# A gate table from one 256-column product per token, gate banks taken before the maximum, and 20 early expert pairs in a two-layer encoder kernel

## The chip, the cores and the metric

The kernel runs on one core of a Trainium2 chip. The metric is the device time of one execution in microseconds (us); before the change it is 2279.7 us, the median of three runs (2278.73 to 2285.3). The engines are named as the profile names them: PE is TensorE, PEld its weight loads, DVE VectorE, ACT ScalarE, POOL GpSimd, SP SyncE, which here only starts DMAs.

## The reference

Two layers over 256 tokens of width 1024, in float32. Each layer has three attention mixers whose outputs are gated and added, and then an expert layer (PEER). The change touches the expert layer most:

```python
def peer(xn, wq, subkeys, u, v):
    q = (xt @ wq).reshape(T, PEER_HEADS, 2, PEER_HALF)
    s = jnp.einsum('thpc,phnc->thpn', q, subkeys)
    top_s, top_i = lax.top_k(s, PEER_TOPK)                      # 16 of 128 keys, twice
    cand_s = top_s[:, :, 0, :, None] + top_s[:, :, 1, None, :]
    cand_i = top_i[:, :, 0, :, None] * N_KEYS + top_i[:, :, 1, None, :]
    best_s, best_pos = lax.top_k(cand_s.reshape(T, PEER_HEADS, 256), PEER_TOPK)
    expert = jnp.take_along_axis(cand_i..., best_pos, axis=-1)  # one of 128 x 128
    g = jax.nn.softmax(best_s, axis=-1)
    hid = jax.nn.gelu(jnp.einsum('td,thkd->thk', xb, u[expert]))
    return jnp.einsum('thk,thkd->td', g * hid, v[expert])
```

The first half of a layer is one projection into q, k, v and gate logits, differential attention (A), band attention (B) and stick-breaking attention (C), `sum_i sigmoid(G_i) * (y_i @ P_i)` and an output projection.

## The kernel before, in words

**Experts as a dense table.** The kernel does not gather experts. It computes the hidden value of all 128 x 128 experts for all 256 tokens and multiplies them by a gate table G[first key (partition), second key, token] that holds the softmax weight of a chosen expert and zero elsewhere. Second keys are worked in 64 pairs; the weights of a pair come as four slots of 128x1024 (two from `w_u`, two from `w_v`).

**Products in halves.** Every big product runs on operands split into a rounded high part and the remainder (type fp32r): `product` (L482 to L486) does hi x hi, lo x hi and hi x lo. So each weight slot is loaded by SP into `raw`, rounded by ACT into `w_hi` (L925, L1107) and subtracted by DVE into `w_lo` (L1253, L1637) or by POOL (L463, L469). There are four slots (`SLOTS`); SP loads a slot again when its w_lo is made.

**The stages of a layer**, each on all engines at once with semaphores (`Signal`, with a count per layer) between them: transposes of x and its gain; 36 projection slots with the C mixer's work and head norms fitted in between (three tables named `between`, one each for PE, ACT and DVE, keyed by slot); 24 gate slots in 16 steps of attention work (two and one in turn, `STEP_SLOTS`); up and output projections; query and scores; then the experts.

**The gate stage.** In step i PE does a gate slot, the score of i + 2, the transposes of probabilities i, in even steps a second gate slot, and mix i - 1 (L687 to L697). On DVE a step is `probabilities(i)`, `score_max(i + 2)` and then `after_gates(i - 1)`, which does the splits of the step's slots and `take_gate` (L1402), the product of a gate bank with rstd. The PE's gate slot waits until the bank two gates before has been taken. All of this runs in the order in which it is written.

**The expert stages.** While DVE chooses the top keys (L1553 to L1608), PE does `EARLY` = 18 pairs with `w_u`; their gelu goes straight into G. Then comes the fill stage of `FILL` = 32 pairs, in which PE alternates one slot of a pair (24 products) with one `gate_group` of four tokens (64 groups in all). For a group DVE builds two rows of 128 zeros and ones for each token (`make_hot`, L1643), ACT multiplies one of them by the token's weight (`weigh_hot`, L1172, four instructions), PE multiplies the two (L801, f32, 128x128 for each token), DVE multiplies the columns whose hidden values stand already in G (`keep`, L1652), and ACT copies the rest (`take_group`, L1186). The gelu of the pair follows (L1198, L1200) and `weigh_fill` (L1661). The 14 late pairs do `w_u` and `w_v` in turn, the remaining 50 (`KEPT`) only `w_v`.

**Between the layers** DVE adds the output to x in four tiles (L1736), PE transposes them, DVE applies the gain (L1262), ACT rounds (L935) and DVE subtracts (L1270); the first product of the layer needs that. At the start of the program SP loads x tiles 0 and 1, and ACT, once tile 1 is there, tiles 2 and 3 (L898 to L900).

## Time and profile before

| | before |
|---|---|
| median of three runs | 2279.7 us |
| profiled execution, its own time | 2281.6 us |
| its span, first to last instruction | 2279.9 us |
| PE busy | 2223.6 us (98%) |
| DVE busy | 1557.9 us (68%) |
| ACT busy | 1175.7 us (52%) |
| POOL busy | 252.1 us (11%) |
| mean granted clock of PE | 0.995 |

Busy time is the union of an engine's instructions; on PE it is modelled from starts, so the starts tell more than the durations. The idle time of PE, some 56 us, is put down to the instruction that released it. A granted clock of 1.00 is 2.4 GHz, 0.50 is 1.2 GHz. The timeline gives each instruction's start and duration; "x4" merges neighbours of one kind, and the value in brackets is the engine's idle time before.

### The profile page before, as it was taken

The numbers are of one execution on the slowest core, as the hardware profiler recorded it, in microseconds if no ns is written. First come the engines' busy times: TensorE is split into PE (matmuls) and PEld (weight loads), VectorE is DVE, ScalarE is ACT, GpSimd is POOL, SyncE is SP. The second block draws the span as 40 slices with busy tenths as digits, with TensorE's granted clock in tenths as the row PEclk, the third lists the DMA queues.
The fourth block names the chain that finished last, engine by engine and source line by source line (L and its number), as shares of the span: only waits on it lengthen the run. The fifth ranks groups of instructions, "written<-read, shape, count | busy, mean of one in ns | idle before, by whom it ended". The sixth has DMA issues, their size and how long they took to land.

```text
span 2279.9 us, 42254 instructions
## 1 busy us (share of the span) xinstructions
PE 2223.6 (98%) x14628; PEld 2018.3 (89%) x14628; DVE 1557.9 (68%) x2530; ACT 1175.7 (52%) x1932; POOL 252.1 (11%) x154
## 2 busy tenths in 40 slices
PE   8998999999999999999999989999999999999999
PEld 6777999999999998888877879999999999988887
DVE  5756767987776556666567568589777765566665
ACT  5744545477775433333366435454777744433333
POOL 1300006810000000000022000068100000000000
PEclk9999999999999999999999999999999999999999
DMA  6433554544445556656554335545444455556564
GB/s 227 139 130 112 180 181 148 182 142 138 138 138 161 189 184 187 197 188 199 193 185 148 111 112 185 182 143 174 148 138 138 140 165 188 187 186 196 191 195 155
DMA packets 103766, 377.27 MB, mean 165 GB/s; under 512 B 11761, under 2 KB 11761, under 8 KB 103153
## 3 DMA queue, kind: packets, MB, share of 16 engines
q1 hardware_dynamic: 102240, 370.72, 49.8%
q10 hardware_dynamic: 1424, 5.32, 0.7%
q8 instruction: 50, 0.82, 0.1%
q14 instruction: 52, 0.42, 0.1%
HBM read 374.94 MB, written 1.05 MB: 165 GB/s over the span
## 4 chain that ended last, share of the span: by engine, by line
PE 81%; DVE 14%; ACT 3%; issue 2%; DMA 0%; ACTq 0%; DVEq 0%; SPq 0%
PE ps L484 25%; PE ps L485 24%; PE ps L486 24%; PE ps L801 5%; DVE w_lo L1253 2%; DVE arena L1559 1%; PE ps L493 1%; DVE arena L1562 1%; DVE arena L1553 1%; DVE arena L1604 1%; DVE ps L1600 1%; DVE arena L1565 1%; DVE arena L1556 1%; ACT w_hi L925 1%; DVE arena L1608 1%
## 5 line engine op out<-in xcount | busy, mean ns | idle before, releaser
L484 PE MATMUL ps<-hT_hi,w_hi 128*128 128x256 f32 x2688 | 779.9, 290 | 20.0 <-DVE arena L1402 15.6
L1107 ACT ACTIVATE w_hi<-raw 128x1024 fp32r<-128x1024 f32 x512 | 521.0, 1054 | 513.7 <-PE ps L486 511.8
L486 PE MATMUL ps<-hT_hi,w_lo 128*128 128x256 f32 x2688 | 764.1, 284 | 0.0
L485 PE MATMUL ps<-hT_lo,w_hi 128*128 128x256 f32 x2688 | 764.1, 284 | 0.0
L1637 DVE TENSOR_TENSOR w_lo<-raw,w_hi 128x1024 fp32r<-128x1024 f32 x436 | 518.9, 1220 | 109.7 <-ACT w_hi L1107 109.7
L484 PEld LDWEIGHTS ps<-hT_hi,w_hi 128*128 128x128 f32 x2688 | 519.0, 193 | 25.0 <-DVE w_lo L1253 16.8
L485 PEld LDWEIGHTS ps<-hT_lo,w_hi 128*128 128x128 f32 x2688 | 519.5, 193 | 1.1
L486 PEld LDWEIGHTS ps<-hT_hi,w_lo 128*128 128x128 f32 x2688 | 518.8, 193 | 0.0
L484 PE MATMUL ps<-w_hi,wgt_hi 128*128 128x512 f32 x1024 | 398.9, 390 | 0.5 <-DVE wgt_lo L1696 0.5
L485 PE MATMUL ps<-w_lo,wgt_hi 128*128 128x512 f32 x1024 | 398.7, 389 | 0.0
L486 PE MATMUL ps<-w_hi,wgt_lo 128*128 128x512 f32 x1024 | 398.3, 389 | 0.0
L1253 DVE TENSOR_TENSOR w_lo<-raw,w_hi 128x1024 fp32r<-128x1024 f32 x192 | 239.9, 1257 | 147.9 <-ACT w_hi L925 147.7
L925 ACT ACTIVATE w_hi<-raw 128x1024 fp32r<-128x1024 f32 x192 | 201.5, 1057 | 185.5 <-PE ps L486 182.0
L484 PEld LDWEIGHTS ps<-w_hi,wgt_hi 128*128 128x128 f32 x1024 | 192.3, 188 | 40.8 <-issue 1.3
L486 PEld LDWEIGHTS ps<-w_hi,wgt_lo 128*128 128x128 f32 x1024 | 192.2, 188 | 40.0
L485 PEld LDWEIGHTS ps<-w_lo,wgt_hi 128*128 128x128 f32 x1024 | 192.3, 188 | 38.7
L1172 ACT ACTIVATE hot<-hot,route 128x128 f32<-128x128 f32 x512 | 164.0, 391 | 86.1 <-DVE hot L1643 85.9
L463 POOL TENSOR_TENSOR w_lo<-raw,w_hi 128x1024 fp32r<-128x1024 f32 x72 | 172.1, 2413 | 128.1 <-ACT w_hi L1107 128.1
L1721 DVE CAST wgt_hi<-arena 128x512 fp32r x100 | 42.7, 427 | 188.5 <-PE ps L486 188.4
L1643 DVE TENSOR_TENSOR hot<-iota,route 128x1024 f32<-128x1024 f32 x128 | 155.8, 1219 | 0.0
L801 PE MATMUL ps<-hot 128*128 128x128 f32 x1024 | 135.5, 275 | 2.9 <-ACT hot L1172 2.9
L1652 DVE TENSOR_TENSOR arena<-arena,ps 128x152 f32<-128x152 f32 (+31 forms) x128 | 55.6, 434 | 113.3 <-PE ps L801 113.3
(189 smaller groups left out, 2303.1 us busy)
## 6 DMA issues: line engine op xcount, KB each, us to landing
raw<-in_w_u SPq DMA_DIRECT2D x256, 512.0 KB, 3.3
raw<-in_w_v SPq DMA_DIRECT2D x256, 512.0 KB, 4.1
raw<-in_stream SPq DMA_DIRECT2D x192, 512.0 KB, 3.3
arena<-in_bias ACTq DMA_DIRECT2D x2, 1024.0 KB, 7.1
arena<-in_subk ACTq DMA_DIRECT2D x2, 1024.0 KB, 8.2
out<-x SPq DMA_DIRECT2D x4, 256.0 KB, 2.0
arena<-in_params ACTq DMA_DIRECT2D x2, 283.5 KB, 5.5
x<-in_x SPq DMA_DIRECT2D x2, 256.0 KB, 3.8
```

Source lines behind the costliest of these rows:

```text
L463: nc.gpsimd.tensor_tensor(w_lo[:, i, :], raw[:, i, :], w_hi[:, i, :].bitcast(F), ALU.subtract).then_inc(early_ready.sem, 1)
L484: mm(out_, left[0], right[0], start=start, stop=False, skip_group_check=group)
L485: mm(out_, left[0], right[1], start=False, stop=False, skip_group_check=group)
L486: return mm(out_, left[1], right[0], start=False, stop=stop, skip_group_check=group)
L801: last = mm(ps[:, k, q * P:(q + 1) * P], hot[k][:, 0, q, :], hot[k][:, 1, q, :], start=True, stop=True)
L925: f(w_hi[:, n % SLOTS, :], raw[:, n % SLOTS, :], ACT.Copy).then_inc(hi_ready.sem, 1)
L1107: f(w_hi[:, slot, :], raw[:, slot, :], ACT.Copy).then_inc(hi_ready.sem, 1)
L1172: last = f(row, row, ACT.Copy, scale=route[:, 2, 4 * n + q:4 * n + q + 1])
L1253: v.tensor_tensor(w_lo[:, i % SLOTS, :], raw[:, i % SLOTS, :], w_hi[:, i % SLOTS, :].bitcast(F), ALU.subtract).then_inc(w_ready.sem, 1)
L1637: v.tensor_tensor(w_lo[:, slot, :], raw[:, slot, :], w_hi[:, slot, :].bitcast(F), ALU.subtract).then_inc(w_ready.sem, 1)
L1643: v.tensor_tensor(hot[n % 2][:], iota[:].unsqueeze(1).unsqueeze(1).broadcast_to([P, 2, 4, KEYS]), route[:, 0:2, tokens].unsqueeze(3).broad ...
L1652: v.tensor_tensor(kept, kept, ps[:, n % 2, :].rearrange("p (t j) -> p j t", t=4)[:, top:KEYS, :], ALU.mult).then_inc(kept_done.sem, 1)
```

## The change

- **Gate table.** `hot` holds three rows for each token in fp32r: the row of the first key, the row of the second key weighted with the high half of the weight, and the same row weighted with the low half. PE multiplies the first with the other two in one product of 256 columns, into two banks for each group. ACT copies the low half to `low` (`copy_low`), DVE adds it: `add_kept` in place in PSUM for the columns that `keep` uses, `add_late` into G for the others. `take_group` is gone from ACT. DVE also makes the third row (`make_rest`) and the low weights (`route_rest`). The keys 0 to 127 that `make_hot` compares with and the low weights lie in PSUM bank 6.
- **Splits of the fill stage** move from DVE to POOL (`N_POOL` is 104 instead of 38); DVE keeps those of the last two pairs' loads.
- **20 early pairs** instead of 18, so 12 late ones.
- **Gate stage.** DVE does `after_gates(i - 1)` ahead of `score_max(i + 2)`, and in it `take_gate` ahead of the slot's split. ACT takes transposed probabilities ahead of the next exponents.
- **Projection stage.** `c_later` 0 and 1 and what follows from them come one slot later.
- **SP** has its layer loop written out; it loads all four x tiles, two ahead of stream slot 0 and two ahead of slot 1. The split of the second layer's slot 0 comes after the second x tile at the end of the first layer.
- `diag`, `rstd_b`, `gsum` and `ginv` share the place of `hot`.

```diff
-EARLY = 18
+EARLY = 20
-N_POOL = N_EARLY + 2
+N_POOL = N_EARLY + 2 * FILL
...
+        keys_ps = ps[:, 6, 0:KEYS]
+        route_lo = ps[:, 6, KEYS:KEYS + T]
+        g_parts = [ps[:, 4 * k:4 * k + 2, :].rearrange("p a (t s j) -> p (a t) s j", t=2, s=2) for k in range(2)]
...
             # SP
-            for n in range(2):
-                sp.dma_start(x_tile(n), x_in[:, n, 0:512]).then_inc(x_ready[n].sem, 16)
+                for k in range(SLOTS):
+                    if layer == 0 and k < 2:
+                        load_x(2 * k)
+                        load_x(2 * k + 1)
+                    load_stream(0, k)
...
             # POOL
-                with pool.Fori(0, N_EARLY // SLOTS) as r:
+                with pool.Fori(0, N_POOL // SLOTS) as r:
...
             # PE, ACT and DVE tables of the projection stage
-                    17: ((ab_transposes, 0),), 20: ((c_later, 0),), 21: ((c_later, 1), (ab_transposes, 1)),
+                    17: ((ab_transposes, 0),), 21: ((c_later, 0),), 22: ((c_later, 1), (ab_transposes, 1)),
...
             # PE
                 def gate_group(n, k):
                     pe.wait_ge(hot_weighted.sem, hot_weighted.at(layer, n + 1))
-                    pe.wait_ge(g_ready.sem, g_ready.at(layer, n - 1))
+                    pe.wait_ge(kept_done.sem, kept_done.at(layer, n - 1))
                     for q in range(4):
-                        last = mm(ps[:, k, q * P:(q + 1) * P], hot[k][:, 0, q, :], hot[k][:, 1, q, :],
-                                  start=True, stop=True)
+                        last = mm(ps[:, 4 * k + q // 2, (q % 2) * T:(q % 2 + 1) * T], hot[k][:, q, 0, :],
+                                  hot[k][:, q, 1:3, :].rearrange("p a b -> p (a b)"), start=True, stop=True)
...
             # ACT, start
-            act.wait_ge(x_ready[1].sem, 16)
-            for n in range(2, 4):
-                act.dma_start(x_tile(n), x_in[:, n - 2, 512:1024]).then_inc(x_ready[n].sem, 16)
...
             # ACT, gate stage
                 for i in range(16):
+                    if i:
+                        take_probT(i - 1)
                     if i + 1 < 16:
                         exponents_of(i + 1)
                     if i:
-                        take_probT(i - 1)
                         after_gates(i - 1)
...
             # ACT, fill stage
+                def copy_low(n):
+                    act.wait_ge(g_mm.sem, g_mm.at(layer, n + 1))
+                    if n:
+                        act.wait_ge(g_ready.sem, g_ready.at(layer, n))
+                    f(low[:], g_parts[n % 2][:, :, 1, :], ACT.Copy).then_inc(low_copied.sem, 1)
...
                     fill_split(2 * u + 4, fill_mm, 2 * u + 1)
-                    take_group(2 * u)
-                    if u < FILL - 1:
-                        weigh_hot(2 * u + 2)
+                    copy_low(2 * u)
+                    if u:
+                        weigh_hot(2 * u + 1)
                     # the two gelus of the pair stand here, unchanged
                     fill_split(2 * u + 5, fill_mm, 2 * u + 2)
-                    take_group(2 * u + 1)
+                    copy_low(2 * u + 1)
                     if u < FILL - 1:
-                        weigh_hot(2 * u + 3)
+                        weigh_hot(2 * u + 2)
...
             # DVE, gate stage
                     for n in range(STEP_FROM[i], STEP_FROM[i + 1]):
-                        split((N_QKV + n + SLOTS,))
                         if n % 2:
                             take_gate(n // 2)
+                        split((N_QKV + n + SLOTS,))
...
                     probabilities(i)
+                    if i:
+                        after_gates(i - 1)
                     if i + 2 < 16:
                         score_max(i + 2)
-                    if i:
-                        after_gates(i - 1)
...
             # DVE, fill stage
                 def make_hot(n):
+                    own.one(v.tensor_tensor(hot[n % 2][:, :, 0:2, :],
+                                            keys_ps.unsqueeze(1).unsqueeze(1).broadcast_to([P, 4, 2, KEYS]),
+                                            route[:, 0:2, tokens]..., ALU.is_equal).then_inc(dve_chain, 1))
+                def make_rest(n):
+                    v.tensor_tensor(hot[n % 2][:, :, 2, :], hot[n % 2][:, :, 1, :].bitcast(F),
+                                    route_lo[:, tokens]..., ALU.mult).then_inc(hot_ready.sem, 1)
+                def add_kept(n):
+                    dve.wait_ge(low_copied.sem, low_copied.at(layer, n + 1))
+                    own.one(v.tensor_tensor(high, high, low[:, :, top:KEYS], ALU.add).then_inc(dve_chain, 1))
+                def add_late(n):
+                    v.tensor_tensor(G[:, 0:top, 4 * n:4 * n + 4], ..., low[...], ALU.add).then_inc(g_ready.sem, 1)
...
                 for u in range(FILL):
-                    keep(2 * u)
-                    if not last_pair:
-                        make_hot(2 * u + 2)
-                    split_e(N_FILL + 2 * u + 3, (2 * u + 3) % SLOTS)
-                    keep(2 * u + 1)
-                    if not last_pair:
-                        make_hot(2 * u + 3)
+                    for n in (2 * u, 2 * u + 1):
+                        add_kept(n)
+                        add_late(n)
+                        if not last_pair:
+                            make_hot(n + 2)
+                        keep(n)
+                        if not last_pair:
+                            make_rest(n + 2)
                     weigh_fill(u)
-                    if not last_pair:
-                        split_e(N_FILL + 2 * u + 4, (2 * u + 4) % SLOTS)
+                    if u >= FILL - 2:
+                        split_e(N_LATE + u - (FILL - 2), u - (FILL - 2))
...
             # DVE, end of a layer
+                    if n == 1 and layer + 1 < LAYERS:
+                        split((0,), layer + 1)
```

## Rows read from the trace of the kernel before

**Rows 1.** The page: busy us, share of the span, instructions

```profile
PE 2223.6 (98%) x14628; PEld 2018.3 (89%) x14628; DVE 1557.9 (68%) x2530; ACT 1175.7 (52%) x1932; POOL 252.1 (11%) x154
```

**Rows 2.** Waits of PE: us in total, times, longest

```profile
PE ps L484 <- DVE arena L1402: 15.6, 6, 2.9
PE ps L493 <- DMA x<-in_x: 9.2, 3, 4.7
PE ps L493 <- DVE arena L1436: 6.6, 6, 2.0
PE ps L493 <- DVE arena L1342: 2.7, 2, 1.3
PE ps L484 <- ACT arena L1186: 2.3, 2, 1.1
```

**Rows 3.** Stretches, gate stages: length, busy of PE, PEld, DVE, ACT, POOL, clock

```profile
130.00:252.00 122.00, 108.59 (x829) 98.03 (x828) 76.91 (x140) 55.82 (x118) 2.47 (x4) 0.97 0.40 130
1261.00:1383.00 122.00, 108.22 (x793) 97.28 (x792) 72.91 (x134) 51.82 (x116) 2.47 (x4) 0.93 0.38 123
```

**Rows 4.** Timeline of PE, fill stage: start, duration, instruction

```profile
592.34 1.06 PE L801 MATMUL ps<-hot 128*128 128x128 f32 x8
...
593.15 0.36 PE L484 MATMUL ps<-hT_hi,w_hi 128*128 128x256 f32 x1
...
596.11 0.39 PE L801 MATMUL ps<-hot 128*128 128x128 f32 x2
```

**Rows 5.** Timeline of PE and ACT, end of the last fill pair

```profile
708.87 0.28 PE L485 MATMUL ps<-hT_lo,w_hi 128*128 128x256 f32 x1
708.99 0.28 PE L486 MATMUL ps<-hT_hi,w_lo 128*128 128x256 f32 x1
...
709.31 0.58 ACT L1198 ACTIVATE ps<-ps 128x512 f32<-128x512 f32 x1 [2.00 <-PE ps L486]
709.80 1.05 ACT L1107 ACTIVATE w_hi<-raw 128x1024 fp32r<-128x1024 f32 x1
```

**Rows 6.** Timeline of ACT, fill stage

```profile
596.31 0.38 ACT L1198 ACTIVATE ps<-ps 128x272 f32<-128x272 f32 x1
...
596.85 1.06 ACT L1107 ACTIVATE w_hi<-raw 128x1024 fp32r<-128x1024 f32 x1
597.80 0.37 ACT L1186 ACTIVATE arena<-ps 128x240 f32<-128x240 f32 x1
```

**Rows 7.** Timeline of PE, DVE and ACT, start of the fill stage

```profile
469.12 0.55 PE L493 MATMUL ps<-ident,arena 128*128 128x128 f32 x3 [0.79 <-DVE arena L1621]
...
471.08 2.35 DVE L1643 TENSOR_TENSOR hot<-iota,route 128x1024 f32<-128x1024 f32 x2
...
474.08 1.28 ACT L1172 ACTIVATE hot<-hot,route 128x128 f32<-128x128 f32 x4
...
475.48 1.15 PE L801 MATMUL ps<-hot 128*128 128x128 f32 x8 [0.53 <-ACT hot L1172]
```

**Rows 8.** DVE and POOL groups by shape: count, busy us, mean ns, idle before

```profile
L1604 DVE TENSOR_TENSOR arena<-ps,arena 128x2048 f32<-128x2048 f32 x8 | 18.3, 2292 | 0.3
...
L1583 DVE TENSOR_TENSOR arena<-arena 128x128 f32<-128x128 f32 x4 | 8.3, 2066 | 0.1
...
L1337 DVE TENSOR_TENSOR arena<-arena 128x128 f32<-128x128 f32 x16 | 4.0, 290 | 0.3
...
L463 POOL TENSOR_TENSOR w_lo<-raw,w_hi 128x1024 fp32r<-128x1024 f32 x72 | 172.1, 2413 | 128.1 <-ACT w_hi L1107 128.1
```

**Rows 9.** Timeline of DVE and PE, gate stage; last a stretch as in rows 3

```profile
160.74 0.69 DVE L1421 SCALAR_TENSOR_TENSOR arena<-ps,blockmask 128x512 f32<-128x512 f32 x1 [3.75 <-PE ps L611]
...
164.01 0.38 PE L484 MATMUL ps<-hT_hi,w_hi 128*128 128x256 f32 x1 [2.91 <-DVE arena L1402]
...
166.00:168.00 2.00, 2.00 (x12) 2.00 (x11) 0.12 (x1) 0.00 (x0) 0.00 (x0) 0.50 0.82 252
```

**Rows 10.** Timeline of DVE between the layers

```profile
1143.06 1.22 DVE L1253 TENSOR_TENSOR w_lo<-raw,w_hi 128x1024 fp32r<-128x1024 f32 x1
```

More of the change, by code:

```diff
@@ L43 @@
 N_LAYER = N_STREAM + 4 * PAIRS
[L44 removed]
+N_POOL = N_EARLY + 2 * FILL
 N_DVE = N_LAYER - N_POOL
[L46 to L47 removed]
+N_LATE = N_STREAM
 N_V = N_LATE + 4 * LATE
@@ L464, in _ @@
                                                 ).then_inc(early_ready.sem, 1)
-                for e in range(2):
-                    pool.wait_ge(hi_ready.sem, hi_ready.at(layer, N_STREAM + N_EARLY + e + 1))
-                    pool.sem_inc(seen_pool, 1)
-                    nc.gpsimd.tensor_tensor(w_lo[:, e, :], raw[:, e, :], w_hi[:, e, :].bitcast(F), ALU.subtract
-                                            ).then_inc(early_ready.sem, 1)
                 pool.wait_ge(pool_chain, own.n)
@@ L893, in _ @@
             own = Count()
-            for s in (g_ready, gelu_ready, hi_ready, early_gelu):
+            for s in (gelu_ready, hi_ready, early_gelu):
                 act.sem_inc(s.sem, s.start)
@@ L1170, in weigh_hot @@
                     for q in range(4):
-                        row = hot[n % 2][:, 0, q, :]
-                        last = f(row, row, ACT.Copy, scale=route[:, 2, 4 * n + q:4 * n + q + 1])
+                        row = hot[n % 2][:, q, 1, :]
+                        last = f(row, row.bitcast(F), ACT.Copy, scale=route_hi[:, 4 * n + q:4 * n + q + 1].bitcast(F))
                     last.then_inc(hot_weighted.sem, 1)
@@ L1248, in _, with split @@
             for layer in range(LAYERS):
-                def split(n):
+                def split(n, layer=layer):
                     for i in n:
@@ L1289, in _ @@
                 gain_tiles(0, (0, 1))
-                split((0,))
+                if layer == 0:
+                    split((0,))
                 rest_tiles(0, (0, 1))
@@ L1647, in keep @@
+                def add_late(n):
+                    top = fill_key(n // 2 - 1)
+                    v.tensor_tensor(G[:, 0:top, 4 * n:4 * n + 4],
+                                    g_parts[n % 2][:, :, 0, :].rearrange("p t j -> p j t")[:, 0:top, :],
+                                    low[:].rearrange("p t j -> p j t")[:, 0:top, :], ALU.add).then_inc(g_ready.sem, 1)
                 def keep(n):
-                    dve.wait_ge(g_mm.sem, g_mm.at(layer, n + 1))
+                    dve.wait_ge(dve_chain, made[-1])
@@ L1662, in weigh_fill, with route_rest @@
                                     ALU.mult).then_inc(fill_used.sem, 1)
-                split_e(N_FILL + 2, 2)
-                dve.wait_ge(route_ready.sem, route_ready.at(layer, 1))
-                dve.sem_inc(seen_dve, 1)
-                for n in range(2):
-                    make_hot(n)
-                dve.wait_ge(route_ready.sem, route_ready.at(layer, 2))
-                dve.sem_inc(seen_dve, 1)
+                def route_rest(t):
+                    dve.wait_ge(route_ready.sem, route_ready.at(layer, t + 1))
+                    own.one(v.tensor_tensor(route_lo[:, t * P:(t + 1) * P], route_ps(t)[:, 2 * P:3 * P],
+                                            route_hi[:, t * P:(t + 1) * P].bitcast(F), ALU.subtract).then_inc(dve_chain, 1))
+                own.one(v.tensor_copy(keys_ps, iota[:]).then_inc(dve_chain, 1))
+                route_rest(0)
+                dve.wait_ge(dve_chain, own.n)
+                make_hot(0)
+                make_rest(0)
+                make_hot(1)
+                route_rest(1)
+                make_rest(1)
+                dve.wait_ge(dve_chain, own.n)
                 dve.wait_ge(early_gelu.sem, early_gelu.at(layer, EARLY))
```

90 lines of the change are left out of this document (44 added, 46 removed).

## The prediction

> **What bounds the kernel now.** I read the busy shares of the page first [rows 1]: TensorE (PE) is busy for 2223.6 of 2279.9 us, so a gain can come only from less PE work, from its 56 idle us, or from a clock that falls. The view of waits shows where most of the idle time lies [rows 2]: 15.6 us for the gate banks (L1402), 6.6 us for the probabilities (L1436), 2.7 us for the rotated heads, 9.2 us for x at the start. The stretch view shows that the gate and softmax stage holds almost half of it, and a low clock beside it: 122 us with 108.59 busy at a granted clock of 0.97, and 122 with 108.22 at 0.93 in the second layer [rows 3]. In the fill stage PE never waits, VectorE (DVE) and ScalarE (ACT) wait for it, so there the price of each product on PE is the time.
>
> **Gate table, work on PE.** One group (four tokens) starts at 592.34, the next slot's first product at 593.15, the next group at 596.11 [rows 4]: 0.81 + 2.96 = 3.77 us for each slot of 24 products with its group, 7.54 a pair. Products of the slot start 0.12 apart (708.87, 708.99) [rows 5]. A new group is four products of 256 columns in fp32r, the form of the slot's own products, so 4 x 0.12 = 0.48, and the slot's first product no longer follows an fp32 one: 28 x 0.12 = 3.36, 6.72 a pair. If PE stays the bound, that is 0.82 us a pair, and 31 pairs in each of two layers give 51 us. The Trainium skill (FP8 and Floating Point Precision, TensorE Precision Notes) says that true FP32 takes four passes through the array. The group's 0.81 us against 0.48 for twice the columns agrees with that: four passes of 128 columns against one of 256.
>
> **Gate table, what ACT then has to do.** Write Z for the start of the last product of a pair's second slot. ACT can start its gelu at Z + 0.32 (708.99, then 709.31) and its next instruction 0.49 later [rows 5]; in mid-stage the two gelus take 0.54 together and the split 0.95 (596.31, 596.85, 597.80) [rows 6]. Before, the weights of a hot group came a whole slot ahead. Now the order behind the gelu is: split, copy_low (128x512 out of PSUM, for which I take the 0.49 of the gelu of that shape), then four weighings, 1.28 us, and PE starts 0.12 us after their end (474.08 + 1.28, then 475.48) [rows 7]. Sum: 0.32 + 0.54 + 0.95 + 0.49 + 1.28 + 0.12 = 3.70. PE itself reaches that group at Z + 0.12 + 0.48 + 2.88 = Z + 3.48. So PE stalls 0.22 us in every pair; the first product after a halt costs some 0.08 more (2.96 against 24 x 0.12). Period: 3.70 + 0.56 + 2.76 = 7.02. The other half of the pair has slack: ACT's split 0.95, copy 0.49 and weighing 1.28 begin at 0.32 past a slot of 2.88. I take 7.02, a gain of 0.52 a pair.
>
> **Gate table, what DVE has to do.** Its pair is two make_hot of 1.22 (two in 2.35, so each overlaps 0.08 with the next), two make_rest of 0.69 (512 elements), and the rest follows from 0.17 + 1.03 per thousand elements (1024: 1.22 [rows 7], 512: 0.69 [rows 9]): the adds 2 x 0.87, the keeps 0.33 to 0.59 each, weigh_fill 0.19 to 0.69. That is 6.4 in the first and 7.4 in the last pair, 0.9 less for eleven overlaps: 5.5 to 6.5, under 7.02. The loop group done, copy_low, two adds, make_hot, keep, make_rest, weighing is 0.3 + 0.6 + 0.75 + 1.14 + 0.4 + 0.7 + 1.3 = 5.2 and also fits. The splits that leave DVE go to GpSimd (POOL) at 2.41 each, 4.8 in 7.02.
> Does POOL stop DVE? One row says it can: L1583, 128x128 with both inputs in SBUF, takes 2066 ns on average while POOL subtracts, where 290 ns is usual for that shape (L1337). But L1604, one input in PSUM, keeps 2292 ns for 2048 elements at the same time [rows 8]. All the fill stage's new DVE work has one input in PSUM (the keys and the low route are moved there), so I price this at nothing; the two splits left for DVE come when POOL is done. The Trainium skill (SBUF — State Buffer, Who interferes with whom) has the rule: two SBUF inputs of VectorE contend with a GpSimd instruction that reads SBUF, one input doesn't. The trace agrees, with those two rows.
>
> **Edges of the fill stage.** At its start the chain for groups 0 and 1 is longer: route copies 0.5, route_rest 0.3, make_hot 1.22, make_rest 0.69, weighing 1.28, and the second group waits for another copy, rest and weighing. By the same durations pair 1 starts 8.1 us after the first route transposes. Its group 2 waits some 2.1 us, since DVE starts its adds only after copy_low(0), so its Z is at 8.1 + 2.88 + 2.1 + 0.56 + 2.76 = 16.4. Z of pair 31 is 30 periods of 7.02 on, and the late stage starts 3.25 after it, since it waits for gelu, split, copy_low and two DVE adds: 230.2 us in all. Before, Z of pair 31 is 708.99 - 469.12 = 239.9 after the transposes [rows 5, 7], and the late stage follows after 0.12, the last group of 0.89 and a wait of 1.1 [rows 2]: 242.0. With the wait of 0.8 before the transposes, which two more early pairs (96 products of 0.12, 11.5 us of PE work) cover, a layer gains 12.6. Halts of 2 to 3 us also halved the clock (below), which I put at 1 to 2 us a layer. **Fill: 21 us in both layers**, with 44 (no stall, PE the bound) and 8 (ACT 0.2 us a pair slower than I think) as bounds. Moving two pairs from late to early changes no PE product: nothing.
>
> **Gate banks ahead of the maximum.** In the timeline DVE idles 3.75 us until 160.74 for the next score, then does maximum, split and only then the bank's product with rstd; PE's gate slot starts at 164.01, after 2.91 idle, and from 166 to 168 the granted clock is 0.50 [rows 9]. With the new order take_gate and the splits run in those 3.75 us. What is late next: the score behind it. The maximum (1.4) follows PE's score as soon as before, and the next probabilities come right after it instead of after 1.8 to 2.9 us of splits and take, so the waits on the probabilities go too. Over two steps DVE has 9.3 us of work (twice some 1.2 for probabilities and 1.3 for a maximum, three splits of 1.13, one and a half takes of 0.6) and PE 10.7 (three slots of 2.88 and about 1 us a step of scores, transposes and mixes). I keep 2.5 us a layer of the 13.4 and 13.8 idle us for the first scores and the tail: 22 back. The clock: 3% and 7% of 122 us are 12.2 us, less 1.7 while PE stood idle: 10.5 back, if no halt of 2 us is left. Bounds: 27 + 10.5, and half, 16. The Trainium skill (TensorE: Matmul & The Clock Gate, What's actually happening) has two levels, 1.2 and 2.4 GHz, the lower one after idle time. The row agrees: 0.50, the lower level, behind a halt of 2.91 us.
>
> **The smaller parts.** c_later one slot later: the 2.7 us on L1342 go, and a smaller wait on c_keep with it, new ones may come; 3.5 (0 to 4.3). Split (0) ahead of the layer's end: its 1.22 us at 1143.06 no longer stand between the gains and hT_lo [rows 10], once: 0.9 (0 to 1.1). x tiles 2 and 3 issued at once by SP instead of behind ACT's wait: its longest wait of 4.7 us [rows 2] goes, but the second stream slot comes behind them and ACT's split (1) stands ahead of its rounding; 1.5 (-1 to 3). Written-out layers on SP: loads are issued long ahead, nothing.
>
> **Sum.** 21 + 22 + 10.5 + 3.5 + 0.9 + 1.5 = 59.4. The profiled execution took 2281.6 us by its own time, 1.7 more than its span and 1.9 above the median of 2279.7. So 2222.2 for such an execution, 2220 as the median.
>
> **Rivals.** A: PE stays the bound in the fill stage, since ACT overlaps more than I add up. For it: ACT and DVE both have idle time in every pair of before. Against: four of the six terms are starts read off the timeline. 44 instead of 21: 2197. B: the gate stage gives half, since a wait on the splits (which now stand ahead of the maximum and themselves wait for ACT) replaces the old one and the clock still falls. For it: DVE's 9.3 of 10.7 is tight. 16 instead of 32.5: 2237. C, the slower one: POOL and DVE exclude each other in the fill stage although one input is in PSUM. A pair would cost 5.9 of DVE and 4.8 of POOL, 10.7 us in turn: 3.2 us more than before, 62 times, 196 us, less the 38 of the other parts: 2438. It decides above 7.54 + 38/62 = 8.15 a pair. Against it stands L1604 at 2292 ns. D: the 256-column product is no cheaper than the old one, or the order costs as much on ACT: fill 0, 2241.
>
> **How the numbers follow.** Mine 0.50, A 0.20, B 0.18, D 0.07, C 0.03, others 0.02. The range is 2190 (A with everything else at its upper end) to 2248 (B, with fill at its lower bound). Measurement tells 0.3%, 7 us, from none. All cases but C are faster by more: faster 0.94, same 0.02, slower 0.04.
>
> **What would show it.** In the profile after: groups of L801 as 128x256, four to a group, starting 0.12 apart; a wait of PE on the weighing in every pair of about 0.2 us and a pair of 7.0 us (6.7 for A); copy_low near 0.59; POOL's subtraction at 2.41 and make_hot at 1.22 though both run (longer for C); no wait on L1402's line above 1 us and a clock of 1.00 in both gate stages (B: a wait on L1253 or the maximum). Wrong at the root it would be if copy_low or the weighing took other durations than the rows I lent them.

## The result and the profile after

The changed kernel takes 2222.8 us (median of four runs, 2222.1 to 2224.0) where the kernel before took 2281.2 beside it: a ratio of 0.9743, 95% interval 0.9726 to 0.976. That is 58.4 us less; forecast were 59.4 off the profiled execution and 2220 us. The profiled execution of after took 2224.0 us, its span is 2222.3.

The page of the kernel after: busy us, share of the span, instructions (compare [rows 1]).

```profile
PE 2184.6 (98%) x14116; PEld 1968.4 (89%) x14116; DVE 1591.6 (72%) x2784; ACT 1197.9 (54%) x1936; POOL 570.6 (26%) x286
```

Waits of PE of the kernel after: us in total, times, longest (compare [rows 2]).

```profile
PE ps L806 <- ACT hot L1172: 6.9, 5, 2.0
PE ps L498 <- DMA x<-in_x: 6.3, 3, 4.7
PE ps L489 <- DVE arena L1670: 5.1, 2, 2.6
PE ps L589 <- DVE arena L1373: 4.7, 2, 2.3
PE ps L489 <- DVE hT_lo L1269: 3.4, 2, 2.6
PE ps L616 <- DVE arena L1424: 1.6, 4, 0.5
...
PE ps L498 <- DVE arena L1436: 0.8, 2, 0.4
```

The 15.6 us for the gate banks are gone, the probabilities (L1436) are down from 6.6 to 0.8. Longer than before are the waits at the start of the fill stage (L806 <- L1172, 1.2 and 2.0 us in each layer where it was 0.9 and 0.5) and the one at its end (L1670, 2.6 us instead of 1.1). New are two stalls of 2.3 us in the projection stage (L1373). The gate stages of both layers as stretches (compare [rows 3]; columns as there):

```profile
130.00:252.00 122.00, 120.69 (x953) 110.28 (x952) 89.19 (x152) 66.59 (x126) 2.47 (x4) 1.00 0.45 150
1230.00:1352.00 122.00, 120.69 (x954) 109.68 (x952) 87.90 (x149) 66.05 (x128) 2.47 (x4) 1.00 0.44 148
```

PE is busy for 120.69 of 122 us at full clock, where it was 108.59 at 0.97 and 108.22 at 0.93. Last, the critical place of a fill pair, PE, ACT and POOL (compare [rows 4 to 6]):

```profile
591.54 0.73 PE L806 MATMUL ps<-hot 128*128 128x256 f32 x4
...
592.83 2.41 POOL L474 TENSOR_TENSOR w_lo<-raw,w_hi 128x1024 fp32r<-128x1024 f32 x1 [0.51 <-ACT w_hi L1107]
594.86 0.28 PE L491 MATMUL ps<-hT_hi,w_lo 128*128 128x256 f32 x1
...
595.18 0.40 ACT L1197 ACTIVATE ps<-ps 128x288 f32<-128x288 f32 x1 [0.59 <-PE ps L491]
595.49 0.35 ACT L1199 ACTIVATE arena<-ps 128x224 f32<-128x224 f32 x1
595.73 1.06 ACT L1107 ACTIVATE w_hi<-raw 128x1024 fp32r<-128x1024 f32 x1
596.68 0.60 ACT L1187 ACTIVATE low<-ps 128x512 f32<-128x512 f32 x1
597.15 1.28 ACT L1172 ACTIVATE hot<-hot,route_hi 128x128 fp32r<-128x128 f32 x4
...
598.59 0.74 PE L806 MATMUL ps<-hot 128*128 128x256 f32 x4
```

The pair is 598.59 - 591.54 = 7.05 us long; forecast was 7.02. With Z at 594.86, ACT's chain runs as written in the prediction: gelu at Z + 0.32, split 0.55 later, copy_low 0.95 on, weighing 0.47 on and 1.28 long. PE starts at Z + 3.73 (forecast 3.70), where it could have at Z + 3.48.

Between landmarks that both traces have (starts of PE's first instruction of a stage), in us:

| stretch | before | after | difference | forecast |
|---|---|---|---|---|
| to the first product | 13.05 | 13.26 | +0.2 | -1.5 |
| to the first score, both layers | 115.11, 114.60 | 117.97, 114.51 | +2.8 | -3.5 |
| gate stage, projections and query, to the first product of query and keys | 224.96, 229.06 | 208.63, 208.62 | -36.8 | -32.5 |
| to the route transposes | 116.00, 116.00 | 125.22, 125.23 | +18.5 | +21.4 |
| fill, to the first late product | 242.18, 242.17 | 231.90, 231.89 | -20.6 | -19.4 |
| to layer 2's first product; to the last product | 433.63, 429.46 | 423.50, 417.89 | -21.7 | -23.9 |

The sum is -57.6. The forecast's fill term of 21 is spread over two rows here: 1.6 are the waits ahead of the transposes, which stand in the fourth row with the 23.0 us of four more early pairs. The last row holds the same 23.0 for four fewer late ones and the 0.9 of split (0).

### The profile page after: what moved, and what is told of

The parts are those of the page before. It is cut to its first block, busy times and chain, and to the rows that moved or that the text cites. A ratio compares the mean times of both kernels' runs of the same rounds, so it can differ in the third digit from the quotient of the medians.

```text
span 2222.3 us, 41570 instructions
## 1 busy us (share of the span) xinstructions
PE 2184.6 (98%) x14116; PEld 1968.4 (89%) x14116; DVE 1591.6 (72%) x2784; ACT 1197.9 (54%) x1936; POOL 570.6 (26%) x286
## 4 chain that ended last, share of the span: by engine, by line
PE 94%; DVE 3%; ACT 2%; issue 1%; DMA 0%; SPq 0%; ACTq 0%; DVEq 0%
PE ps L489 29%; PE ps L490 28%; PE ps L491 28%; PE ps L806 3%; PE ps L498 1%; DVE w_lo L1252 1%; PE ps L616 1%; PE ps L775 1%; ACT w_hi L924 1%; PE ps L577 0%; DMA raw<-in_stream 0%; PE ps L589 0%; PE ps L687 0%; DVE arena L1353 0%; ACT hot L1172 0%
## 5 line engine op out<-in xcount | busy, mean ns | idle before, releaser
L489 PE MATMUL ps<-hT_hi,w_hi 128*128 128x256 f32 x2688 | 770.5, 287 | 5.1 <-DVE arena L1670 5.1
L474 POOL TENSOR_TENSOR w_lo<-raw,w_hi 128x1024 fp32r<-128x1024 f32 x208 | 498.8, 2407 | 272.5 <-ACT w_hi L1107 272.5
L1637 DVE TENSOR_TENSOR w_lo<-raw,w_hi 128x1024 fp32r<-128x1024 f32 x304 | 358.2, 1220 | 91.2 <-ACT w_hi L1107 91.2
L1252 DVE TENSOR_TENSOR w_lo<-raw,w_hi 128x1024 fp32r<-128x1024 f32 x192 | 239.0, 1251 | 166.6 <-ACT w_hi L924 166.3
L1172 ACT ACTIVATE hot<-hot,route_hi 128x128 fp32r<-128x128 f32 x512 | 164.1, 398 | 20.5 <-DVE hot L1655 19.5
L1645 DVE TENSOR_TENSOR hot<-ps,route 128x1024 fp32r<-128x1024 f32 x128 | 156.1, 1220 | 0.1
L489 PE MATMUL ps<-w_hi,hT_hi 128*128 128x512 f32 x288 | 119.1, 414 | 3.4 <-DVE hT_lo L1269 3.4
```

The lines of the kernel that those rows point to most:

```text
L474: nc.gpsimd.tensor_tensor(w_lo[:, i, :], raw[:, i, :], w_hi[:, i, :].bitcast(F), ALU.subtract).then_inc(early_ready.sem, 1)
L489: mm(out_, left[0], right[0], start=start, stop=False, skip_group_check=group)
L1172: last = f(row, row.bitcast(F), ACT.Copy, scale=route_hi[:, 4 * n + q:4 * n + q + 1].bitcast(F))
L1252: v.tensor_tensor(w_lo[:, i % SLOTS, :], raw[:, i % SLOTS, :], w_hi[:, i % SLOTS, :].bitcast(F), ALU.subtract).then_inc(w_ready.sem, 1)
L1637: v.tensor_tensor(w_lo[:, slot, :], raw[:, slot, :], w_hi[:, slot, :].bitcast(F), ALU.subtract).then_inc(w_ready.sem, 1)
L1645: own.one(v.tensor_tensor(hot[n % 2][:, :, 0:2, :], keys_ps.unsqueeze(1).unsqueeze(1).broadcast_to([P, 4, 2, KEYS]), route[:, 0:2, tokens] ...
```

## The experiments

**1. Is it ACT's chain that sets the period of a fill pair?** Rival A said that PE would.

```diff
                     last.then_inc(fill_gelu.sem, 1)
-                    fill_split(2 * u + 5, fill_mm, 2 * u + 2)
                     copy_low(2 * u + 1)
                     if u < FILL - 1:
                         weigh_hot(2 * u + 2)
+                    fill_split(2 * u + 5, fill_mm, 2 * u + 2)
```

> The changed kernel, with one edit: in the second half of a pair ACT does copy_low and the four weighings for the next group ahead of the rounding of the next weight slot (fill_split), instead of behind it. Theory (ACT's chain behind the gelu sets the period): Z + 0.32 + 0.54 + 0.60 + 1.28 + 0.12 = Z + 2.86 is ready before PE gets there at Z + 3.48, so the period falls from 7.05 to 6.72 us and the time by 62 x 0.33 = 20 us, to about 2203 us. Rival (the period is set by DVE's adds and make_hot, or by PE itself with its records inexact): the period stays at 7.05 and the time at 2223. Second rival: the rounding, now 1.9 us later, is what PE waits for, since POOL's 2.4 us of subtraction follows it: the period is over 7.05 and the time above 2223.

Measured: 2206.2 us (2205.1 to 2206.8), 16.5 less than the changed kernel. PE of this kernel in mid-stage:

```profile
590.66 0.64 PE L806 MATMUL ps<-hot 128*128 128x256 f32 x4
594.02 0.64 PE L806 MATMUL ps<-hot 128*128 128x256 f32 x4
597.38 0.64 PE L806 MATMUL ps<-hot 128*128 128x256 f32 x4
```

Groups are 3.36 us apart, so the pair is 6.72: PE is the bound, as soon as 0.95 us leave the chain. The theory holds. Of the 20 us 3.5 are missing, since in most of the stage every fourth gap is 3.50 instead of 3.36 (600.91 follows 597.38, and 614.48 follows 610.99); some 31 such gaps in two layers make 4 us. They come once in a turn of PE's loop over two pairs, but experiment 7 has the same loop and no such gap (3.77 throughout), so what holds PE there stays open.

**2. The gate stage's order, undone in the changed kernel; 11. the same order alone, in the kernel before.**

```diff
 # ACT
-                    if i:
-                        take_probT(i - 1)
                     if i + 1 < 16:
                         exponents_of(i + 1)
                     if i:
+                        take_probT(i - 1)
                         after_gates(i - 1)
 # DVE
+                        split((N_QKV + n + SLOTS,))
                         if n % 2:
                             take_gate(n // 2)
-                        split((N_QKV + n + SLOTS,))
...
                     probabilities(i)
-                    if i:
-                        after_gates(i - 1)
                     if i + 2 < 16:
                         score_max(i + 2)
+                    if i:
+                        after_gates(i - 1)
```

> The changed kernel with the gate stage in its old order: on DVE score_max ahead of after_gates and the split ahead of take_gate, on ACT the exponents ahead of the transposed probabilities. Theory (this order alone gives what the gate stages gained, halts and clock): first score to first query product 225 and 229 us again instead of 208.6 twice, so 37 us slower, 2259 us, with granted clocks of 0.97 and 0.93 back. Rival (a part of the 37 us came from c_later or from another edit that shifts the phase): 15 to 30 us slower.

> The kernel before with only the gate stage's new order on DVE and ACT. Theory (the gate stage's gain doesn't hang on the fill stage or on c_later): 37 us less than 2281, as much as undoing it in the changed kernel cost, 2244. Rival (the new order needs c_later's shift or the new start to get its phase): 2250 to 2260.

Measured: 2260.0 us (2258.0 to 2263.0), 37.2 more than the changed kernel, and, alone in the kernel before, 2245.5 (2245.4 to 2246.3) against 2280.1, 34.7 less. Waits of PE with the order undone:

```profile
PE ps L489 <- DVE arena L1401: 15.2, 6, 2.9
...
PE ps L498 <- DVE arena L1435: 6.6, 6, 2.0
```

They are those of [rows 2]. The stretches of both gate stages had a granted clock of 0.97; the kernel before had 0.97 and 0.93, so the low clock came back, in the second layer not to its full depth. With the order alone in the kernel before:

```profile
130.00:252.00 122.00, 120.69 (x963) 111.04 (x962) 91.50 (x154) 66.23 (x126) 2.47 (x4) 1.00 0.46 152
```

So the stage's gain of 35 to 37 us comes from this order and hangs on nothing else of the change.

**8. Which half of the order does it?** The diff of experiment 2 without its middle part, so that `take_gate` stays ahead of the slot's split (DVE's part is shown; ACT has its old order, as in experiment 2):

```diff
                         if n % 2:
                             take_gate(n // 2)
                         split((N_QKV + n + SLOTS,))
...
                     probabilities(i)
-                    if i:
-                        after_gates(i - 1)
                     if i + 2 < 16:
                         score_max(i + 2)
+                    if i:
+                        after_gates(i - 1)
```

> The changed kernel with the gate stage's old order but for one edit: take_gate stays ahead of the split. Theory (what PE waits for is the product of the bank, behind maximum, split and take in turn): of the 2.9 us halt some 1.2 us, one split, go in each of the six halts on this line, and with halts of 1.7 us part of the low clock stays: 10 to 18 us of the 37, so 2241 to 2250. Rival (the whole chain has only to be a little shorter for the halts to vanish): 30 us or more, under 2230. Second rival (the order maximum first is all): 2258.

Measured: 2248.0 us (2247.1 to 2249.9), so this edit alone is worth 12 of the 37 us. Waits of PE:

```profile
PE ps L489 <- DVE arena L1401: 8.4, 6, 1.8
...
PE ps L498 <- DVE arena L1435: 6.6, 6, 2.0
```

The halts for the bank are 1.8 instead of 2.9 us long, one split less, as expected. The waits on the probabilities stay. They and the other 25 us go with the rest of the order: `after_gates` ahead of `score_max` on DVE, and ACT's transposed probabilities ahead of the exponents. Which of these two does it, or whether both are needed, no run shows.

**3 and 6. c_later one slot later.** Experiment 3 takes the shift back on PE, ACT and DVE. Experiment 6, on top of experiment 1, takes it back on DVE alone:

```diff
 # PE's table (experiment 3)
-                    17: ((ab_transposes, 0),), 21: ((c_later, 0),), 22: ((c_later, 1), (ab_transposes, 1)),
+                    17: ((ab_transposes, 0),), 20: ((c_later, 0),), 21: ((c_later, 1), (ab_transposes, 1)),
 # ACT's table (experiment 3)
-                    18: ((take_ab_transposes, 0),), 23: ((c_weights, 0), (take_ab_transposes, 1)),
-                    24: ((c_weights, 1),), 25: ((c_weights, 2),), 26: ((c_weights, 3), (take_ab_transposes, 2)),
+                    18: ((take_ab_transposes, 0),), 22: ((take_ab_transposes, 1), (c_weights, 0)),
+                    23: ((c_weights, 1),), 25: ((c_weights, 2),), 26: ((c_weights, 3), (take_ab_transposes, 2)),
 # DVE's table (experiments 3 and 6)
-                    22: ((c_take_later, 0), (head_norm, 4)), 23: ((c_take_later, 1), (head_norm, 5)),
-                    24: ((c_take_later, 2), (head_block, 3)), 25: ((c_take_later, 3), (c_mask, 0)),
-                    26: ((c_take_later, 4), (head_norm, 6), (c_mask, 1)),
+                    21: ((c_take_later, 0), (head_norm, 4)), 22: ((c_take_later, 1), (head_norm, 5)),
+                    24: ((c_take_later, 2), (head_block, 3), (c_mask, 0)), 25: ((c_take_later, 3), (c_mask, 1)),
+                    26: ((c_take_later, 4), (head_norm, 6)),
```

> The changed kernel with c_later and what follows from it one slot earlier again, as in the kernel before. Theory: shifting them cost more than it gave in the first layer, because c_take_later(0) now stands on DVE behind the split of slot 26 and PE waits 2.3 us for it with a clock of 0.83 after it. Without the shift the waits of 0.7 and 1.3 us on L1368 and L1342 come back in each layer, the 2.3 us ones and the slow stretch go: 1 to 4 us faster, about 2220. Rival (as I predicted, the shift brings 1.75 us a layer, and the stall of 2.3 us is made by something else, such as a phase shift of the weight slots from the later start): 1 to 4 us slower, about 2226, with the stall of L589 gone or not.

> On top of the first experiment: PE and ACT keep c_later in the new slots, but DVE does c_take_later and c_mask in the places of the kernel before, so c_take_later(0) stands ahead of the subtraction of slot 26. Theory (the 2.3 us stall of c_later(2) comes from that place): the stall goes, the waits on L1342 and L1368 stay away, 2.3 us and the slow stretch less in each layer, 4 to 5 us faster than 2206, about 2202. Rival: DVE now waits for c_later(0) and c_later(1) itself, with the subtraction of the weight slot behind it, and PE pays the same later: 2206.

Measured: experiment 3 takes 2223.0 us (2222.0 to 2224.6), no difference from the changed kernel: neither the 1 to 4 us faster of my theory nor the 1 to 4 us slower of the rival. Waits of PE of experiment 3, and a stretch of it (length, busy of PE, clock, DMA share, GB/s):

```profile
PE ps L498 <- DVE arena L1342: 2.7, 2, 1.3
...
PE ps L589 <- DVE arena L1368: 1.3, 2, 0.7
```

```profile
88.00:100.00 12.00, 11.20 (x49) 1.00 0.39 133
```

The same stretch of the changed kernel, and its timeline of DVE and PE:

```profile
88.00:100.00 12.00, 9.67 (x36) 0.86 0.50 164
```

```profile
94.05 0.69 DVE L1373 TENSOR_TENSOR arena<-arena,ps 128x512 f32<-128x512 f32 x1
...
94.79 1.12 PE L589 MATMUL ps<-arena 128*128 128x512 f32 x2 [2.33 <-DVE arena L1373]
```

The shift trades 4.0 us of waits for 4.7 and a low clock in the first layer. The first score comes at 131.23 us with it and at 129.84 without. In the two profiled executions the last stretch gives the 1.4 us back: from the late stage of the second layer on it takes 419.2 us without the shift and 417.9 with it, and its first 20 us have a granted clock of 0.93 without the shift. The edit changes nothing in that stage, so the profiles can't say whether the shift itself costs those 1.4 us; by the medians it costs nothing that can be measured. Experiment 6 takes 2202.2 us (2201.5 to 2202.8), 4.0 less than experiment 1; its wait on this line:

```profile
PE ps L589 <- DVE arena L1373: 2.4, 2, 1.2
```

The stall is halved, not gone as I expected; the old waits do not return. So its cause is the place of `c_take_later(0)` on DVE, behind two splits in a row (91.79 to 94.05 us): one has left, 1.13 us of DVE's time, and the other still stands ahead of it and of the 1.2 us halt that is left.

**4. POOL beside DVE.** `make_hot` compares with the keys in SBUF instead of PSUM.

```diff
                     own.one(v.tensor_tensor(hot[n % 2][:, :, 0:2, :],
-                                            keys_ps.unsqueeze(1).unsqueeze(1).broadcast_to([P, 4, 2, KEYS]),
+                                            iota[:].unsqueeze(1).unsqueeze(1).broadcast_to([P, 4, 2, KEYS]),
```

> The changed kernel, but make_hot compares with the keys in SBUF, so that both its inputs lie in SBUF while POOL subtracts beside it. Theory (two SBUF inputs exclude a POOL subtraction, one input in PSUM does not): make_hot is held while POOL works, its mean rises from 1.22 us to 2 us or more, DVE's pair from 5.9 to over 7.5 us, the period from 7.05 to 8 to 9 us, 2290 to 2340 us. Rival (place of the keys makes no difference, the 2.07 us seen on L1583 had another cause): make_hot stays near 1.22 us and the time at 2223.

Measured: 2257.0 us (2255.6 to 2259.6), 34 more. The timeline of DVE and POOL of this kernel, and a stretch of its fill stage (columns as in [rows 3]):

```profile
590.08 2.41 POOL L474 TENSOR_TENSOR w_lo<-raw,w_hi 128x1024 fp32r<-128x1024 f32 x1 [1.51 <-ACT w_hi L1107]
...
591.37 2.19 DVE L1645 TENSOR_TENSOR hot<-iota,route 128x1024 fp32r<-128x1024 f32 x1
...
593.43 2.40 POOL L474 TENSOR_TENSOR w_lo<-raw,w_hi 128x1024 fp32r<-128x1024 f32 x1 [0.95 <-ACT w_hi L1107]
...
595.60 1.32 DVE L1645 TENSOR_TENSOR hot<-iota,route 128x1024 fp32r<-128x1024 f32 x1
```

```profile
490.00:690.00 200.00, 192.52 (x1495) 181.84 (x1494) 200.00 (x296) 164.13 (x376) 129.15 (x54) 1.00 0.41 140
```

The first `make_hot` starts while POOL works, and ends 1.07 us after POOL's end at 592.49; the second meets only the last 0.23 us of POOL's. The mean over all 128 is 1.85 us against 1.22, and DVE is busy for 200 of 200 us: it has become the bound. The same instruction with one input in PSUM kept 1.22 us beside the same subtraction. The rule of the Trainium skill that the prediction drew on (SBUF — State Buffer, Who interferes with whom) calls the shared port pair an exclusive lock. The trace agrees: the instruction that came second ended 1.07 us after POOL's end, close to the 1.22 us that it takes alone. What I overrated is the price: the period rose to some 7.5 us, not to 8 to 9, since only the part of `make_hot` that meets POOL waits.

**7. Is it the type or the width that makes the new product cheap?** On top of experiment 1, two products of 128 columns for each token.

```diff
-                        last = mm(ps[:, 4 * k + q // 2, (q % 2) * T:(q % 2 + 1) * T], hot[k][:, q, 0, :],
-                                  hot[k][:, q, 1:3, :].rearrange("p a b -> p (a b)"), start=True, stop=True)
+                        for j in range(2):
+                            last = mm(ps[:, 4 * k + q // 2, (q % 2) * T + j * P:(q % 2) * T + (j + 1) * P],
+                                      hot[k][:, q, 0, :], hot[k][:, q, 1 + j, :], start=True, stop=True)
```

> On top of the first experiment: each token's product of 256 columns is written as two products of 128 columns in the same type (fp32r), eight to a group instead of four. Theory (the old form of 128 columns was dear since 128 columns of f32 took 0.10 us, and its price lies in the type, not in the width): a product of 128 columns of fp32r takes 0.06 us and the group stays near 0.48; the time at 2206 to 2210, since a few hundredths more per instruction add up. Rival (a width of 256 is what makes the type cheap): eight products of 0.10 or more, group 0.81 or above, 0.33 us in each of 128 groups, 42 us more, 2248 or above.

Measured: 2252.0 us (2250.7 to 2254.3), 45.8 more than experiment 1: my theory fell.

```profile
592.18 1.01 PE L807 MATMUL ps<-hot 128*128 128x128 f32 x8
593.03 0.33 PE L489 MATMUL ps<-hT_hi,w_hi 128*128 128x256 f32 x1
...
595.95 1.01 PE L807 MATMUL ps<-hot 128*128 128x128 f32 x8
```

Eight products take 0.85 us, 0.106 each on average, where one of 256 columns takes 0.12. The average flatters them, since the first gap is only 0.06 us: the records of single instructions start 0.112 us apart within the group, and so do the weight loads, of which each product has its own. The period is 2 x 3.77 = 7.54, that of the kernel before to the hundredth. Half the width saves some 7% of the distance between products, so the number of products counts. The old group, too, stands in the trace as eight instructions of 128 columns, in 0.81 us [rows 4], and their starts and loads are 0.112 us apart as well, in another type. The Trainium skill (TensorE: Matmul & The Clock Gate, LDWEIGHTS) prices a load of 128 weight columns at 128 / 1.2 = 107 ns; the 0.112 lie 5% above it. That fits the loads as what sets the distance, but no run changed the load alone, so this is argued and not shown. The "four passes of 128 columns" of my prediction are not refuted, but the count of instructions explains the same row.

**5 and 12. The start.** Experiment 12 gives x tiles 2 and 3 back to ACT in the changed kernel. Experiment 5, on top of experiment 1, changes ACT's order:

```diff
                 split(0)
-                split(1)
                 round_tiles(0, (0, 1))
+                split(1)
```

and experiment 12 is this:

```diff
 # SP
-                    if layer == 0 and k < 2:
+                    if layer == 0 and k < 1:
                         load_x(2 * k)
                         load_x(2 * k + 1)
 # ACT, start
+            act.wait_ge(x_ready[1].sem, 16)
+            for n in range(2, 4):
+                act.dma_start(x_tile(n), x_in[:, n - 2, 512:1024]).then_inc(x_ready[n].sem, 16)
```

> On top of the first experiment (weighing ahead of the rounding of the weight slot): at a layer's start ACT rounds x tiles 0 and 1 ahead of weight slot 1 instead of behind it. Theory (the gain of 2.9 us from the earlier x tiles was eaten by ACT standing 2.37 us on the landing of weight slot 1 with the rounding of x behind it): hT_lo is ready 2.3 us earlier, the first product starts at 11.0 instead of 13.26 us, 1.5 to 2.3 us faster than 2206, about 2204. Rival (DVE's subtraction of slot 0 or the landing of slot 1 itself is next and costs the same): the first product starts earlier but the second slot halts PE, time unchanged at 2206.

> The changed kernel with x tiles 2 and 3 loaded by ACT once tile 1 is there, as before, and not by SP ahead of weight slot 1. Theory (from the trace: the first product started at 13.26 us after the change and at 13.05 before): loading them early pays nothing at the first product, since it puts weight slot 1 later and ACT's rounding of x stands behind that; the time stays within 1 us of 2223. Rival (as I predicted): 1.5 us slower, 2224 to 2225.

Measured: experiment 12 takes 2223.7 us (2222.7 to 2226.1), not told apart from the changed kernel's 2222.8; its first product starts at 13.83. Experiment 5 takes 2203.2 (2200.0 to 2204.2), 3.0 less than experiment 1. ACT and PE, first in the changed kernel, then in experiment 5:

```profile
10.90 1.06 ACT L924 ACTIVATE w_hi<-raw 128x1024 fp32r<-128x1024 f32 x1 [2.37 <-DMA raw<-in_stream]
11.87 1.13 ACT L934 ACTIVATE hT_hi<-arena 128x512 fp32r<-128x512 f32 x2
...
13.26 0.80 PE L489 MATMUL ps<-w_hi,hT_hi 128*128 128x512 f32 x1 [2.56 <-DVE hT_lo L1269]
```

```profile
8.53 1.13 ACT L934 ACTIVATE hT_hi<-arena 128x512 fp32r<-128x512 f32 x2
...
10.54 0.79 PE L489 MATMUL ps<-w_hi,hT_hi 128*128 128x512 f32 x1
11.00 1.06 ACT L924 ACTIVATE w_hi<-raw 128x1024 fp32r<-128x1024 f32 x1 [1.34 <-DMA raw<-in_stream]
```

In the changed kernel x tiles 0 and 1 wait for their rounding while ACT stands for weight slot 1. With the order turned, PE starts 2.7 us earlier. Another part of the start lies ahead of that: the transposes of x tile 0 start at 4.70 us in the changed kernel, at 4.87 in experiment 12 and at 4.13 in the kernel before, so tile 0 lands some 0.6 us later under the new order of loads.

**10. 18 early pairs instead of 20**, in the changed kernel.

```diff
-EARLY = 20
+EARLY = 18
```

> The changed kernel with 18 early pairs and 14 late ones instead of 20 and 12. Theory (two pairs moved from late to early change no PE product, and their cover of the wait for the route columns is small: 0.8 us a layer that was seen before the change): 1 to 3 us slower, 2224 to 2226. From the landmarks (early part 9.2 us longer in each layer, late part 9.1 and 11.6 us shorter) 1.1 us a layer, 2225. Rival (early pairs are dearer than late ones, as their gelu adds work beside the choice of keys): faster, 2220.

Measured: 2233.9 us (2232.6 to 2235.3), 11.1 more: I expected 1 to 3. Waits of PE that are longer or new in this kernel, and ACT's timeline:

```profile
PE ps L806 <- ACT hot L1172: 9.1, 5, 2.5
...
PE ps L498 <- DVE arena L1621: 2.9, 2, 1.5
PE ps L489 <- POOL w_lo L474: 2.2, 2, 1.1
```

```profile
439.25 0.31 ACT L1151 ACTIVATE arena<-arena 128x128 f32<-128x128 f32 x1 [2.56 <-DVE arena L1583]
439.58 1.28 ACT L1140 ACT_TABLE_LOAD   x1
440.88 0.60 ACT L1140 ACTIVATE arena<-ps 128x512 f32<-128x512 f32 x1
```

The route columns come 1.5 us too late for PE in each layer, the first weighed group 1.3 us more, and ACT stands 2.56 us for the exponents of the routing (L1151, behind DVE's L1583) with the rounding of the next weight slots behind them, so POOL is late and PE halts 1.1 us. With 20 early pairs ACT comes to the same place later and waits for nothing. Together 7.3 of the 10.9 us of span. The halt behind POOL is not new: the kernel before, also with 18 early pairs, has it too.

```profile
PE ps L484 <- POOL w_lo L463: 2.2, 2, 1.1
```

The clock's share is uneven: in the second layer the stretch from 1790 to 1810 us is granted 0.83 here and 1.00 in the changed kernel, but in the first layer the stretch from 680 to 700 us is granted 1.00 here and 0.92 in the changed kernel. Between landmarks 8.8 of the 10.9 us lie in the early and fill stages and 1.7 in the late ones, where the two clocks differ.

**9. The three better orders together**: the diffs of experiments 1 and 5, and of 6 on DVE's table.

> The changed kernel with the three orders of experiments 1, 5 and 6 together: ACT weighs ahead of rounding the weight slot in the fill stage, rounds x tiles 0 and 1 ahead of weight slot 1, and DVE does c_take_later at its old places. Theory (three stalls at three places, independent): 2206.2 - 3.0 - 4.0 = 2199 us. Rival (the later part of the program is bound by something that the earlier start only fills, such as the weight transfers): 2202 to 2204.

Measured: 2198.5 us (2197.8 to 2199.5), a ratio to the kernel before of 0.9641 (0.9628 to 0.9654). The gains add up (forecast 2199). It beats both kernels: 24 us under the changed one, 82 under the one before.

## Why the prediction was right, and where its steps were not

The total came within 3 us. The two mechanisms that carry it, the gate banks ahead of the maximum and the chain of ACT in a fill pair, are as forecast. That the total came so close is partly luck, since errors of some 10 us in two other terms cancel.

**Gate stage.** Forecast 22 us of idle time and 10.5 of clock, 32.5; measured 36.8 between landmarks, 34.7 and 37.2 by experiments 11 and 2. The mechanism is the forecast one. The term was too small in both parts. I kept 2.5 us a layer of idle time and 1.3 are left (122 less 120.69), so 24.6 us of idle time came back instead of 22 (PE's busy time in the two stretches rose from 216.8 to 241.4). The other 12.2 of the 36.8 are the clock, where I had taken 1.7 off and forecast 10.5. Rival B, half of the gain, is out.

**Fill stage, inside.** The chain of six terms gave 7.02 us, the trace 7.05, and experiment 1 shows that the terms are the cause: without the split's 0.95 the pair is 6.72. Only PE's start had to be read as Z + 3.73 instead of 3.70. Rival A would have needed the order of experiment 1. The largest lent duration held: `copy_low` 0.47 to the next start against 0.49. Rival C was priced at nothing by L1604 [rows 8]; POOL's subtraction stays at 2.41 and `make_hot` at 1.22. Experiment 4 shows that the place of the keys is what keeps it out, though its price in this stage is 34 us for the keys alone, not my 196 for everything.

**Fill stage, edges, and the early pairs.** The stretch fits (20.6 against 19.4), yet "moving two pairs changes nothing" was the wrong step: by experiment 10 it is worth 11.1 us, not the 1.6 that I had given it inside the fill term. Without the move the fill stage takes 233.3 us a layer (455.39 to 688.73), 1.4 more, and the stretches around it lose the rest. I had looked at one wait, 0.8 us (L1621), and not at the halt of 1.1 us behind POOL in each layer (L463), which stood in the same view, nor at the fact that the faster fill's chain, route copies, `make_rest` and weighing, stands behind the same choice of keys, nor at ACT's wait for it. By the same experiment the gate table with 18 early pairs gives less than I credited. That kernel is 46 us faster than the one before in the same comparison (2280.1 to 2233.9), of which the gate stage's order has 35 to 37 and the small parts nothing: 9 to 11 are left for the table, against a term of 21 less the 1.6. Between landmarks the table comes to 13: its fill stretches are 17.7 us shorter than before; the stretches ahead of them are 1.3 us longer, and the late ones 3.1; the projection stages lose the rest. Behind the halt at the end of the second fill stage (2.7 us) the last stretch takes 432.1 us where it took 429.5, with the clock of 0.83. No run has the table alone, so this is a difference of kernels and not a measurement of it. So a term that was too large by 6 to 10 and one that was too small by 9 to 11 stand in a sum that looks right. That is luck.

**Smaller parts.** c_later: forecast 3.5 us less, measured nothing by experiment 3, and 2.8 more between the landmarks. The waits that I named went; what failed is "new ones may come", which I left at its lower bound of 0 although `c_take_later(0)` goes behind one more split of DVE, and that order can be read off the diff. Start: forecast 1.5 less, measured 0.2 more and 0.6 less in two comparisons, so nothing; I had named ACT's split (1) ahead of its rounding and priced it too low (experiment 5: 2.7). The halt of 4.7 us for x tiles 2 and 3 did go (the 4.7 in the waits after is the start of the program). Split (0) between the layers: the x transposes start after 0.92 us idle instead of 0.20 and the first product follows 1.1 us sooner; next to nothing is left of 0.9 (4.13 us from the last product of the first layer to the first of the second, where it was 4.18). Together these three terms, 5.9 us in the sum, brought none; the 4.3 more of the gate stage stand against them, which is luck as well.

**Range.** By its own terms the upper end (rival B with fill at 8) is 2279.7 - 16 - 8 - 5.9 = 2250, not 2248. It changes nothing here.

## What to carry over

- In a loop of several engines, add up what each engine still has to do between the product that releases it and the product that waits for it, in its program order. The sum told the period to 0.03 us, and it names the instruction to move: the one nobody is waiting for yet.
- An instruction that is moved one place later goes behind everything that now stands ahead of it on its engine; look there for the wait that replaces the one removed, and look at work "only moved" for what it covers.
- When a sum comes out right, undo its parts one by one: here one term of 0 was worth 11 us, and a term of 21 some 6 to 10 less than it said.

## What was not expected of the hardware

- Products of 128 columns in fp32r start 0.112 us apart and products of 256 columns 0.12 us apart, with a weight load for each; the f32 instructions of 128 columns before were 0.112 us apart too. Splitting a product in two costs 0.37 us for a group of four tokens, 46 us in all.
- In experiment 4 a `make_hot` with both inputs in SBUF that starts during GpSimd's subtraction takes that subtraction's rest and then 1.1 us of its own. With one input in PSUM all 128 take 1.20 to 1.25 us, beside the same subtractions.
- In experiment 1 every fourth gap between groups is 0.14 us longer than the others. This stays open. The kernel before, with x tiles 2 and 3 loaded by ACT, starts its first product at 13.05 us and experiment 12 at 13.83: nearly all of that is there from the first x transposes on (4.13 and 4.87), and why tile 0 lands later is open.
